# Output weights of a hybrid decoder step: split on chip one stage earlier, tokens' blocks stored by tiles, the samples' steps moved forward

## The chip, the cores and the metric

One core of a Trainium2 chip runs the whole kernel. The metric is the device time of one execution in microseconds; with one core that is the core's own time. The engines are TensorE (PE, matmuls), VectorE (DVE), ScalarE (ACT), GpSimd (POOL) and SyncE (SP, which here issues the DMAs). Each runs its own instruction stream strictly in order, and they meet only at semaphores.

## The reference, cut to what matters

Two layers over a prompt of 2048 tokens, and in the same launch one decode step for 8 samples (1 token each, with their own caches). All fp32.

```
D_MODEL 1024, D_MAIN 1024, D_MEMW 512 (4 heads of 128, 256 memory slots), D_CAT 1536, WINDOW 128
for l in (0, 1):
    u, g_main, q_mem, g_mem = split(rmsnorm(x) @ w_in[l])          # 1024 -> 3072
    l == 0: y = rglru(causal_conv4(u))                             # gates by 64x64 block diagonals, linear scan
    l == 1: k, v = rmsnorm(x) @ w_kv; y = sliding_window_gqa(rope(u), rope(k), v, sinks)
    om = softmax(q_mem @ mem_k[l].T) @ mem_v[l]
    z = concat(y * silu(g_main), om * silu(g_mem))                 # 1536
    x = x + z @ w_out[l]                                           # 1536 -> 1024
return rmsnorm(x), and the states and caches (of the prompt and of the samples)
```

## The kernel before, in words

Every large fp32 product is made of three matmuls on rounded halves: with a = a_hi + a_lo and b = b_hi + b_lo (ACT copies to the rounded type, DVE or POOL subtracts for the low part) it sums hi·hi, hi·lo and lo·hi. All PE times below are those of such triples. The program of each engine is written out by hand: stage functions loop over chunks of 512 tokens (`q` counts them) and call hooks of the neighbouring stages (`ahead[...]`), so that work of the next stage is issued between the chunks of this one. A wait stands in the queue of its engine until it is met, and everything behind it stands too.

Stages in order of time: memory keys and values; layer 0's items (`mem_*`, then `lru_*`, the recurrence stage: chunks q = 0 to 33, 12.2 us each, four chunks for each block of 256 weight columns, an "item"); the output product of layer 0 (`output(l=0)`, PE at L2098); layer 1's keys and values, memory items and window attention; and last `paired`, the output product of layer 1 (L2661).

**Recurrence stage.** SP's order in a chunk is `lru_sp` (L1024): tiles, `sums_sp`, weights, rows, then every fourth chunk the load of an item's weights (1 MB, L571) and of the gates' blocks, then the store of a finished z chunk (L677) and of the samples' row. The item's weights are wanted by PE at the second chunk of the next item, for the samples' row of the projection (`project_samples`, L628). ACT's order is `lru_act`: root, weight halves, branch copy, tiles, tanh and exp, gate copy, then `ahead["weights_act"]`. Beside it `block_sums` (L2694) prepares sums of blocks of w_out for the last stage: a step loads two rows of blocks (L2715), POOL makes four sums in place (L2725 to L2730), SP stores them (L2719). There are 6 steps, each over two chunks: in an even chunk SP waits for the previous store to land and issues the loads, in the odd chunk it waits for POOL and stores. From chunk 28 on SP also loads the output weights of layer 0 in thirds (L1782), ACT splits them (L1787).

**Last stage.** The product 1536 -> 1024 is split in two phases f of 768 rows each, and in each phase the 2x2 block product (tokens x rows by rows x columns) is made by seven products of blocks (Winograd's form), of 3 x 3 matmuls of 128x128 by 128x512, about 2.05 us each, in the order P2, P1, P4, P6, P5, P7, P3. A unit is 256 tokens of one phase: units 0 to 7 are phase 0, units 8 to 15 phase 1, and units 0 and 1 are partly woven into the end of the window attention (`tail`; first P2 and P1 of unit 0). For a unit SP loads z in four blocks (A22, S2 = A21, A11, A12; L2284) and x or the partial result (L2293); POOL makes S1, S3, S2, S4 from them (L2402 to L2409); ACT rounds the first three blocks and then the other four (L2440, L2443); DVE makes the low parts in three pieces (L2527), and adds each product from its bank to the rows (L2541). A product may start when the bank was added two products ago (`product`, L2640). In phase 0 the rows go back to DRAM (`store_x`, L2327), in phase 1 they are normalised and stored as the result (`store_y`). z of a unit takes the buffer of the unit two before, and is loaded when that unit's P6 is done. z lies in DRAM as (12, 128, 2048), so a load of a tile is made of pieces of 512 B. The products' weights are loaded raw (a block of w_out, or a sum), rounded by ACT (L2434) and split by DVE (L2520; POOL for P3, L2414): for phase 0 in chunks 29 to 32 of the window stage, for phase 1 in units 3 to 9.

Between the products of units 9 to 13 PE, DVE, ACT and POOL do the window attention of the 8 samples in six steps (`sm[...]`): SP loads rows, keys (L1452) and values (L1476), PE's window scores are L1532. At the end the samples' z is multiplied by w_out, which SP loads again in two halves (`again`, L2336; PE at L2671).

SP's order in a unit is `sync` (L2338): z of the next unit, store of the previous rows (only from unit 9 here), x of the next unit, special loads, and in units 1 to 7 the store of this unit's rows at its end.

## Time and profile before

| | |
|---|---|
| time, median of 3 runs | 2081.75 us (2080.78 to 2083.16) |
| the profiled execution: time, span | 2081.3 us, 2079.5 us |
| PE busy | 2025.7 us (97%), 14353 matmuls |
| DVE, ACT, POOL busy | 1293.0 (62%), 951.7 (46%), 240.0 us (12%) |
| mean granted clock of TensorE | 0.988 of full speed |
| last stage's matmuls, L2661 | 404.6 us in 1008 matmuls, 27.0 us of idle before them |
| DMA | 244.76 MB, 118 GB/s over the span, 251 in the busiest late slice |

The span runs from the first to the last instruction of the profiled execution; the time of that execution is 1.8 us more. With PE busy for 97% of it, what an edit can give is the idle time of PE and the time in which its clock was granted at half.

### The profile page before, as it was taken

Reading aid. Unit: us, or ns where it says so; the run is one execution under the profiler, and the core shown is the slowest. Engines: PE = TensorE matmul, PEld = TensorE weight load, DVE = VectorE, ACT = ScalarE, POOL = GpSimd, SP = SyncE. Lnnn points to the kernel's source line nnn. Section 1 sums busy time; section 2 is a strip of 40 time slices with the busy share of each in tenths; the row PEclk is TensorE's granted clock in tenths of the full one; section 3 lists DMA queues with packets and bytes.
Section 4 is the critical chain, followed back from the end, with each engine's and each line's share of the span. In section 5 each row is a group of like instructions: output and inputs, shape, how many; then the busy total and the mean of one; then the engine's idle time right before and its main releaser. Section 6 shows DMA issues by size and latency. Waiting matters only on the chain.

```text
span 2079.5 us, 34876 instructions
## 1 busy us (share of the span) xinstructions
PE 2025.7 (97%) x14353; PEld 1604.3 (77%) x14353; DVE 1293.0 (62%) x2165; ACT 951.7 (46%) x2061; POOL 240.0 (12%) x232
## 2 busy tenths in 40 slices
PE   9999999999999999999999999999999998998995
PEld 8788887777777787777888888777777887776763
DVE  5745437887777832223634444688888889865764
ACT  6633335777777823222533333444444445223431
POOL 0000001320000000000200000222222220223310
PEclk9999999999999999999999999999999999999997
DMA  9311113332111465453211111212222215467674
GB/s 385 138 64 46 62 45 120 129 126 71 45 45 56 160 211 187 147 169 126 79 44 43 37 43 49 80 50 85 70 85 70 85 63 174 170 231 267 221 251 180
DMA packets 133119, 244.76 MB, mean 118 GB/s; under 512 B 14340, under 2 KB 69668, under 8 KB 128472
## 3 DMA queue, kind: packets, MB, share of 16 engines
q1 hardware_dynamic: 132960, 242.54, 34.2%
q8 instruction: 113, 1.85, 0.4%
q14 instruction: 46, 0.38, 0.1%
HBM read 179.40 MB, written 63.16 MB: 117 GB/s over the span
## 4 chain that ended last, share of the span: by engine, by line
PE 85%; DVE 5%; DMA 4%; SPq 2%; issue 2%; POOL 1%; ACT 1%; DVEq 0%; POOLq 0%
PE bank L608 52%; PE bank L2098 12%; PE bank L2661 4%; PE bank L150 2%; PE bank L712 2%; PE bank L1173 2%; PE bank L448 2%; PE bank L1159 2%; PE bank L699 2%; DMA op_zraw<-z_scratch 2%; PE bank L908 1%; SPq L2284 1%; PE bank L628 1%; DVE op_x L2541 1%; PE bank L702 1%
## 5 line engine op out<-in xcount | busy, mean ns | idle before, releaser
L608 PE MATMUL bank<-x_hi,w_hi 128*128 128x512 f32 x1600 | 636.2, 398 | 0.4 <-DVE w_lo L594 0.4
L608 PE MATMUL bank<-x_hi,w_lo 128*128 128x512 f32 x1600 | 624.1, 390 | 0.0
L608 PE MATMUL bank<-x_lo,w_hi 128*128 128x512 f32 x1600 | 623.1, 389 | 0.0
L608 PEld LDWEIGHTS bank<-x_hi,w_hi 128*128 128x128 f32 x1600 | 300.1, 188 | 96.7 <-issue 35.4
L608 PEld LDWEIGHTS bank<-x_hi,w_lo 128*128 128x128 f32 x1600 | 300.3, 188 | 64.6
L608 PEld LDWEIGHTS bank<-x_lo,w_hi 128*128 128x128 f32 x1600 | 300.5, 188 | 60.8 <-issue 0.7
L2661 PE MATMUL bank<-op_whi_p,op_zhi 128*128 128x512 f32 x336 | 136.9, 407 | 27.0 <-DVE op_x L2541 12.6
L2098 PE MATMUL bank<-wo_hi,z_hi 128*128 128x512 f32 x384 | 151.8, 395 | 1.1 <-DVE z_lo L1821 1.1
L2098 PE MATMUL bank<-wo_lo,z_hi 128*128 128x512 f32 x384 | 149.7, 390 | 0.0
L2098 PE MATMUL bank<-wo_hi,z_lo 128*128 128x512 f32 x384 | 149.5, 389 | 0.0
L758 DVE TENSOR_TENSOR it_P_lo<-bank,it_P_hi 128x512 fp32r<-128x512 f32 x64 | 41.2, 686 | 161.6 <-ACT it_P_hi L753 161.6
L1211 ACT ACTIVATE it_X<-it_X,stat 128x128 f32<-128x128 f32 x256 | 99.2, 389 | 91.9 <-DVE stat L1280 91.9
L653 ACT ACTIVATE it_gh<-bank 128x512 f32<-128x512 f32 x96 | 56.8, 592 | 180.7 <-PE bank L608 180.7
L2661 PE MATMUL bank<-op_whi_p,op_zlo 128*128 128x512 f32 x336 | 134.0, 399 | 0.0
L2661 PE MATMUL bank<-op_wlo_p,op_zhi 128*128 128x512 f32 x336 | 133.7, 398 | 0.0
L1337 POOL TENSOR_SCALAR w_raw<-w_raw,prm 128x256 f32<-128x256 f32 x56 | 59.8, 1069 | 546.0 <-PE bank L628 275.3
L2541 DVE TENSOR_TENSOR op_x<-op_x,bank 128x512 f32<-128x512 f32 (+1 forms) x112 | 84.8, 759 | 53.5 <-PE bank L2661 53.2
L1247 DVE TENSOR_TENSOR it_PTs<-bank,tmask 128x512 f32<-128x512 f32 x128 | 79.4, 682 | 57.4 <-PE bank L150 57.2
L2661 PEld LDWEIGHTS bank<-op_whi_p,op_zhi 128*128 128x128 f32 x336 | 64.9, 193 | 45.8 <-issue 18.9
L747 ACT ACTIVATE it_Pm<-bank,stat 128x256 f32<-128x256 f32 x128 | 59.0, 474 | 88.0 <-DVE stat L766 88.0
L2098 PEld LDWEIGHTS bank<-wo_hi,z_hi 128*128 128x128 f32 x384 | 72.0, 188 | 21.3 <-issue 3.8
L586 ACT ACTIVATE w_hi<-w_raw,prm 128x256 fp32r<-128x256 f32 x200 | 85.1, 507 | 0.3 <-PE bank L702 0.3
(363 smaller groups left out, 3216.0 us busy)
## 6 DMA issues: line engine op xcount, KB each, us to landing
w_raw<-in_w_items SPq DMA_DIRECT2D x25, 1024.0 KB, 5.1
z_scratch<-it_gz SPq DMA_DIRECT2D x96, 256.0 KB, 2.6
it_cs<-in_rope SPq DMA_DIRECT2D x32, 512.0 KB, 4.1
op_x<-x_scratch SPq DMA_DIRECT2D x32, 512.0 KB, 4.9
z_raw<-z_scratch SPq DMA_DIRECT2D x16, 768.0 KB, 5.7
op_zraw<-z_scratch SPq DMA_DIRECT2D x64, 192.0 KB, 4.1
in_rows<-in_x_prompt SPq DMA_DIRECT2D x4, 2048.0 KB, 26.7
in_x<-in_x_T SPq DMA_DIRECT2D x4, 2048.0 KB, 27.3
```

The costliest lines, as they stand in the source:

```text
L150: last = nc.tensor.transpose(banks[a][:, 64 * i:64 * i + 64], of(i)[e, :], ident[e, e])
L448: last = nc.tensor.matmul(mk_bank(i)[:, 256 * h:256 * h + 256], s_, r_, start=(k == 0), stop=(k == KT - 1))
L586: nc.scalar.activation(m.w_hi[w % 2][:, k, :], m.w_raw[w % 2][:, k, :], ACT.Copy, scale=m.prm[:, k, gain(w):gain(w) + 1]).then_inc(S["w_hi ...
L608: last = nc.tensor.matmul(ps, s_, r_, start=(k == 0 and q == 0), stop=(k == KT - 1 and q == 2))
L653: nc.scalar.activation(gh[:, :], PG, ACT.Copy, scale=0.5)
L747: nc.scalar.activation(Pm[:, t, :], (S0, S1)[t // 2][:, (t % 2) * M:(t % 2 + 1) * M], ACT.Exp, bias=negm[:, t:t + 1], scale=MEM_SCALE, acc ...
L1211: e = nc.scalar.activation(X[:, j, :], X[:, j, :], ACT.Exp, bias=negm[:, j:j + 1], accum_out=rs[:, j:j + 1])
L1247: r = nc.vector.tensor_tensor(PTs[:, h, a, :].rearrange("p (t b k) -> p t b k", t=4, b=2), by_halves(m.psum, 6, h), m.tmask[:, a, :].rearr ...
L1337: nc.gpsimd.tensor_scalar(raw, raw, m.prm[:, k, gain(w):gain(w) + 1], None, ALU.mult).then_inc(S["zeros"], 1)
L2098: last = nc.tensor.matmul(bank(t, h), s_, r_, start=(first and q == 0), stop=(end and q == 2))
L2541: nc.vector.tensor_tensor(x, x, y, ALU.add).then_inc(xn, 1)
L2661: last = nc.tensor.matmul(bank(u, i), s_[:, k, :], r_[:, k, :], start=(i not in (P6, P7, P3) and k == 0 and q == 0), stop=(k == KQ - 1 and ...
```

## The change

- **Splitting ahead.** `block_sums` now makes a step in every chunk (q = 3 to 8: wait for POOL, store, wait for the landing, load the next) and then, from chunk 8 on, the high and low parts of all 21 weight blocks of phase 0, in pairs over two chunks each: load raw, ACT copies (hook behind `weights_act`), POOL subtracts, SP stores. In the last stage the weights of phase 0 are loaded as two finished parts (`load_w`, f = 0), and their splits on ACT (21), DVE (18) and POOL (3) are gone there.
- **z by tiles.** z's DRAM buffer is (16, 128, 12, 128); a tile's load is contiguous for each partition, a chunk's store is in pieces of 512 B.
- **Order of SP's queue.** z(u+1) is issued ahead of the row stores of unit u-1 and in pieces, each when the product that last read its buffer is done; x(0) goes ahead of P5's weights, P3's parts behind z(1); row stores of units 1 to 7 come after the next z; in phase 1 the weights P7 get a buffer of their own and are loaded in unit 6; the samples' values go behind the rows in unit 10 and not 11; w_out is loaded again in units 12 and 13 and not 13 and 14.
- **DVE and ACT order.** Tokens' low parts of unit 0 move from behind the window stage's last normalisation to before it; P7's round copy goes ahead of the tokens' of unit 9.
- **Samples' steps.** The six steps are moved forward by three to nine products on PE and DVE.

```diff
-        self.z_d = nc.dram_tensor("z_scratch", (NI, 128, T), F32).ap()
+        self.z_d = nc.dram_tensor("z_scratch", (TT, 128, NI, 128), F32).ap()
...
-        s.dma_start(m.z_d[item(kind, i, p) - l, :, c * CH:(c + 1) * CH], gz[g % NG][:, :]).then_inc(stored[g % NG], 16)
+        s.dma_start(m.z_d[4 * c:4 * c + 4, :, item(kind, i, p) - l, :].rearrange("t p e -> p t e"), gz[g % NG][:, :].rearrange("p (t e) -> p t e", t=4)).then_inc(stored[g % NG], 16)
...
             ahead["weights_act"](act, q)
+            ahead["sums_act"](act, q)
...
-        s.dma_start(m.z_raw[slot(t)][:, :, :], m.z_d[:, :, t * 128:(t + 1) * 128].rearrange("k p t -> p k t")).then_inc(z_ld[t % 2], 16)
+        s.dma_start(m.z_raw[slot(t)][:, :, :], m.z_d[t]).then_inc(z_ld[t % 2], 16)
...
+             [V0, V0 + 12 * KB, V0 + 24 * KB, V0 + 36 * KB, WS + 16 * KB, LO + 54 * KB, WS]]
+    at_hi = [[at_lo[f][i] + 6 * KB for i in range(NPROD)] for f in range(2)]
+    at_hi[0][P3], at_hi[1][P7], at_hi[1][P3] = LO + 48 * KB, HI + 21 * KB, HI + 33 * KB
...
     def load_w(s, f, i):
         on, value = loaded[f][i]
+        if f == 0:
+            s.wait_ge(on, value - 32)
+            for part, to in enumerate((w_hi, w_lo)):
+                s.dma_start(to[0][i][:, :, :].bitcast(F32), sums["split"](part, KQ * i, KQ).rearrange("k p n -> p k n")).then_inc(on, 16)
+            return
         s.wait_ge(on, value - 16)
...
     def load_z(s, u):
         f, j, p = phase(u), u % 8, u % 2
         it["z_stored"](s, NCH * (6 * f + 5) + j // 2)
-        if u >= 2:
-            s.wait_ge(mmd, MM0 + made(u - 2, P6))
-        k = 6 * f
-        for e, k, h in ((A22, k + 3, 1), (S2, k, 1), (A11, k, 0), (A12, k + 3, 0)):
-            s.dma_start(z_raw[p][:, e, :, :], m.z_d[k:k + KQ, :, 256 * j + 128 * h:256 * j + 128 * h + 128].rearrange("k p t -> p k t")).then_inc(z_ld[p], 16)
+        for i, e, k, h in ((P2, A12, KQ, 0), (P1, A11, 0, 0), (P4, A22, KQ, 1), (P6, S2, 0, 1)):
+            if u >= 2:
+                s.wait_ge(mmd, MM0 + made(u - 2, i))
+            s.dma_start(z_raw[p][:, e, :, :], m.z_d[2 * j + h, :, 6 * f + k:6 * f + k + KQ, :]).then_inc(z_ld[p], 16)
...
         if q == 31:
             s.wait_ge(*chunk_free(2))
             load_w(s, 0, P6)
+            load_x(s, 0)
             load_w(s, 0, P5)
-            load_x(s, 0)
             load_w(s, 0, P7)
-            load_w(s, 0, P3)
     def late_sp(s, q):
         if q == 32:
             s.wait_ge(*chunk_free(3))
             load_z(s, 1)
+            load_w(s, 0, P3)
             load_x(s, 1)
...
     def sync(s):
-        for u in range(1, UNITS):
-            if 2 <= u < UNITS - 1:
+        for u in range(2, UNITS):
+            if u < UNITS - 1:
                 load_z(s, u + 1)
-            if u >= 9:
+            if u <= 8:
+                store_x(s, u - 1)
+            else:
                 store_y(s, u - 1)
-            if 2 <= u < UNITS - 1:
+            if u < UNITS - 1:
                 load_x(s, u + 1)
             if u == 2:
                 s.wait_ge(*after("z_ready", NI * NCH))
...
             if u in (3, 4, 5):
                 load_w(s, 1, (P1, P4, P6)[u - 3])
             if u == 6:
+                s.wait_ge(*chunk_free(3))
+                load_w(s, 1, P7)
+            if u == 7:
                 load_w(s, 1, P3)
-            if u == 7:
                 s.wait_ge(mmd, MM0 + made(7, P2))
                 load_w(s, 1, P5)
-            if u < 8:
-                store_x(s, u)
             if u == 8:
-                s.wait_ge(mmd, MM0 + made(7, P7))
-                load_w(s, 1, P7)
                 s.wait_ge(mmd, MM0 + NPROD * 8)
                 sm["sp"](s, 0)
                 sm["sp_keys"](s)
             if u == 10:
                 sm["sp"](s, 1)
-            if u == 11:
                 sm["sp"](s, 2)
-            if u == 13:
+            if u == 12:
                 s.wait_ge(sm["signals"]["pv_d"], 2)
                 again(s, range(0, 8, 2))
+            if u == 13:
+                s.wait_ge(sm["zs_r"], sm["zs_0"] + 3)
+                again(s, range(8, NI, 2))
             if u == 14:
                 s.wait_ge(sm["zs_r"], sm["zs_0"] + 3)
                 sm["sp"](s, 6)
-                again(s, range(8, NI, 2))
                 s.dma_start(x_s[0:NS, :], m.x1_d[TT * 128:TA, :]).then_inc(x_ld[2], 16)
...
     def pool(g):
-        sums_tokens(g, 0)
-        sums_tokens(g, 1)
-        low_pool(g, 0)
-        for u in range(2, UNITS):
+        for u in range(UNITS):
             sums_tokens(g, u)
             if u == 9:
-                low_pool(g, 1)
-            if u == 10:
+                for k in range(KQ):
+                    g.wait_ge(whi, W0 + KQ * P3 + k + 1)
+                    nc.gpsimd.tensor_tensor(w_lo[1][P3][:, k, :], w_raw[1][P3][:, k, :], w_hi[1][P3][:, k, :].bitcast(F32), ALU.subtract).then_inc(wlop, 1)
                 sm["pool"](g)
...
     def within_act(act, q):
-        if q in (29, 30):
-            weights_act(act, 0, (P2, P1)[q - 29])
         if q == 31:
             for n in range(2):
                 tokens_act(act, 0, n)
         if q == 32:
             tokens_act(act, 1, 0)
-            weights_act(act, 0, P7)
-            weights_act(act, 0, P3)
...
+            if u == 8:
+                weights_act(act, P7)
             if 2 <= u + 1 < UNITS:
                 tokens_act(act, u + 1, 0)
             if u == 8:
-                for i in (P7, P3):
-                    weights_act(act, 1, i)
+                weights_act(act, P3)
                 nc.scalar.activation(st[:, 63:64], m.eps, ACT.Sqrt, bias=m.eps, scale=1.0)
             if u < UNITS - 1:
                 tokens_act(act, u + 1, 1)
             if 3 <= u < 8:
-                weights_act(act, 1, (P2, P1, P4, P6, P5)[u - 3])
-            if 9 <= u < 13:
-                sm["act"](act, (0, 1, 2, 4)[u - 9])
+                weights_act(act, u - 3)
+            if u == 9:
+                sm["act"](act, 0)
+            if u == 10:
+                sm["act"](act, 1)
+                sm["act"](act, 2)
+            if u == 12:
+                sm["act"](act, 4)
...
     def within_dve(v, q):
         if q == 31:
-            weights_low(v, 0, P4)
+            for n in range(2):
+                tokens_low(v, 0, n)
         if q == 32:
-            weights_low(v, 0, P7)
             add(v, 0, P5)
             tokens_low(v, 1, 0)
     def result_dve(v, q):
+        if q == 31:
+            tokens_low(v, 0, 2)
         if q == 32:
             add(v, 0, P7)
     def behind_dve(v, q):
-        if q in (29, 30):
-            weights_low(v, 0, (P2, P1)[q - 29])
-        if q == 31:
-            for n in range(3):
-                tokens_low(v, 0, n)
         if q == 32:
             tokens_low(v, 1, 1)
             add(v, 0, P3)
+            tokens_low(v, 1, 2)
...
-                if (u, i) == (9, 0):
+                if (u, i) == (8, 6):
                     sm["sum_rows"](v, c)
...
-                step = {(9, 6): 0, (10, 5): 1, (11, 3): 2, (12, 2): 3, (12, 6): 4, (13, 3): 5}.get((u, i))
+                step = {(9, 3): 0, (10, 2): 1, (10, 6): 2, (11, 5): 3, (12, 1): 4, (12, 5): 5}.get((u, i))
...
-            if u % 8 == 0:
-                pe.wait_ge(*((wlop, WP0 + KQ * f + k + 1) if i == P3 else (wlo, W0 + low_at(f, i, k))))
+            if u == 0 and k == 0:
+                pe.wait_ge(*loaded[0][i])
+            if u == 8:
+                pe.wait_ge(*((wlop, WP0 + k + 1) if i == P3 else (wlo, W0 + KQ * i + k + 1)))
...
-                step = {(9, 2): (0, 1), (10, 1): (1, 1), (10, 2): (1, 2), (10, 3): (1, 3), (11, 1): (2, 3), (12, 0): (3, 3), (12, 4): (4, 3), (13, 1): (5, 3)}.get((u, i))
+                step = {(9, 0): (0, 1), (9, 5): (1, 1), (9, 6): (1, 2), (10, 0): (1, 3), (10, 5): (2, 3), (11, 3): (3, 3), (11, 6): (4, 3), (12, 3): (5, 3)}.get((u, i))
...
+    s_d = nc.dram_tensor("split_scratch", (2, NB, 128, 512), F32).ap()
...
+    blocks = [block[k][i] for i in range(7) for k in range(KQ)]
+    PAIRS_ = [range(n, min(n + 2, NB)) for n in range(0, NB, 2)]
+    Q0 = 2 + NT
+    def keep(s, q):
+        if 3 <= q <= Q0:
+            l, f, k = STEPS[q - 3]
+            s.wait_ge(made, 4 * (q - 2))
+            s.dma_start(t_d[l, f, :, k].rearrange("j p e -> p j e"), b[:, :, :]).then_inc(kept, 16)
+            s.wait_ge(kept, 16 * (q - 2) + 16)
+        if q > Q0 and (q - Q0) % 2 == 0 and (q - Q0) // 2 <= len(PAIRS_):
+            n = (q - Q0) // 2 - 1
+            js = PAIRS_[n]
+            s.wait_ge(made, 4 * NT + 2 * n + len(js))
+            for part, x in enumerate((hi, lo)):
+                s.dma_start(s_d[part, js[0]:js[0] + len(js)].rearrange("j p e -> p j e"), x[:, 0:len(js), :].bitcast(F32)).then_inc(kept, 16)
+            s.wait_ge(kept, 16 * NT + 32 * (n + 1) + 16)
     def sp(s, q):
+        keep(s, q)
+        if 2 <= q < Q0:
+            l, f, k = STEPS[q - 2]
+            for j in range(2):
+                s.dma_start(b[:, 2 * j:2 * j + 2, :], A["w_out"][l, 6 * f + KQ * j + k].rearrange("p (j e) -> p j e", j=2)).then_inc(got, 16)
+        elif q >= Q0 and (q - Q0) % 2 == 0 and (q - Q0) // 2 < len(PAIRS_):
+            for j, n in enumerate(PAIRS_[(q - Q0) // 2]):
+                s.dma_start(raw[:, j, :], blocks[n]).then_inc(got, 16)
+    def act(act, q):
+        n = (q - Q0) // 2
+        if q > Q0 and (q - Q0) % 2 == 1 and n < len(PAIRS_):
+            act.wait_ge(got, 16 + 32 * NT + 32 * n + 16 * len(PAIRS_[n]))
+            for j in range(len(PAIRS_[n])):
+                nc.scalar.activation(hi[:, j, :], raw[:, j, :], ACT.Copy).then_inc(high, 1)
...
+        for n in range(NB):
+            g.wait_ge(high, 16 + n + 1)
+            tt(lo[:, n % 2, :], raw[:, n % 2, :], hi[:, n % 2, :].bitcast(F32), ALU.subtract).then_inc(made, 1)
...
```

## Rows read from the trace of the kernel before

**Rows 1.** Waits of PE, 1600 to 2080 us: engine, line, releaser: total, times, longest.

```profile
PE bank L2671 <- DMA op_w_again<-in_w_out: 15.7, 1, 15.7
PE bank L2661 <- DVE op_x L2541: 12.6, 3, 7.2
PE bank L2661 <- issue: 8.5, 1, 8.5
PE bank L2661 <- DVE op_zlo L2527: 4.9, 4, 1.7
```

**Rows 2.** Timeline of PE: start, duration, what [idle before, releaser].

```profile
1802.99 0.50 PE L2661 MATMUL bank<-op_whi_p,op_zhi 128*128 128x512 f32 x1
...
1901.25 0.50 PE L2661 MATMUL bank<-op_whi_p,op_zhi 128*128 128x512 f32 x1 [0.81 <-DVE op_zlo L2527]
```

**Rows 3.** Recurrence stage: timelines of SP, POOL, PE, and landings of L2719 and L571.

```profile
337.63 0.93 SPq L2715 DMA_DIRECT2D sums<-in_w_out  x2
...
342.69 1.75 POOL L2725 TENSOR_TENSOR sums<-sums 128x512 f32<-128x512 f32 x1 [30.79 <-DMA sums<-in_w_out]
...
349.30 0.38 SPq L2719 DMA_DIRECT2D sums_scratch<-sums  x1
...
DMA to landing us min/median/max: 4.0/4.2/4.8
...
409.72 0.33 SPq L571 DMA_DIRECT2D w_raw<-in_w_items  x1
...
DMA to landing us min/median/max: 5.0/5.0/5.0
...
428.22 1.07 PE L628 MATMUL bank<-w_raw,xsg 128*32 128x256 f32 x16
```

**Rows 4.** Around the stage change: SP, landings of L1782, ACT and DVE.

```profile
681.84 0.38 SPq L1782 DMA_DIRECT2D wo_raw<-in_w_out  x1
...
DMA to landing us min/median/max: 8.0/9.0/9.7
...
682.82 3.90 ACT L1787 ACTIVATE wo_hi<-wo_raw 128x1024 fp32r<-128x1024 f32 x4
...
694.97 3.90 ACT L1787 ACTIVATE wo_hi<-wo_raw 128x1024 fp32r<-128x1024 f32 x4
...
703.22 1.76 DVE L1821 TENSOR_TENSOR z_lo<-z_raw,z_hi 128x1536 fp32r<-128x1536 f32 x1 [0.29 <-ACT z_hi L1817]
```

**Rows 5.** Last stage's start: DVE, SP, and a window (PE to POOL, clock, DMA, GB/s).

```profile
1760.03 1.89 DVE L2520 TENSOR_TENSOR op_wlo_p<-op_wraw_p,op_whi_p 128x512 fp32r<-128x512 f32 x3
...
1766.88 1.22 DVE L1290 TENSOR_TENSOR it_X<-it_X,stat 128x1024 f32<-128x1024 f32 x1
...
1768.63 3.09 DVE L2527 TENSOR_TENSOR op_zlo<-op_zraw,op_zhi 128x1152 fp32r<-128x1152 f32 x3
...
1766.99 2.02 SPq L2284 DMA_DIRECT2D op_zraw<-z_scratch  x4
...
1752.00:1758.00 6.00, 5.99 (x99) 4.64 (x98) 6.00 (x10) 4.05 (x4) 0.00 (x0) 1.00 0.99 280
```

**Rows 6.** Timeline of DVE in unit 4.

```profile
1852.63 1.36 DVE L2527 TENSOR_TENSOR op_zlo<-op_zraw,op_zhi 128x1152 fp32r<-128x1152 f32 x1 [3.43 <-POOL op_zraw L2409]
```

**Rows 7.** From unit 8 on: SP, two windows, POOL and PE.

```profile
1906.96 0.81 SPq L2293 DMA_DIRECT2D op_x<-x_scratch  x2
...
1915.12 3.81 SPq L1452 DMA_DIRECT2D sm_k<-in_cache_mem_k  x8
...
1919.20:1923.00 3.80, 3.80 (x9) 3.02 (x10) 3.71 (x3) 3.44 (x4) 3.80 (x3) 0.50 1.03 410
1930.60:1932.40 1.80, 1.80 (x11) 1.44 (x9) 1.76 (x4) 0.00 (x0) 0.00 (x0) 1.00 1.13 297
...
1934.26 1.41 POOL L2402 TENSOR_TENSOR op_zraw<-op_zraw 128x384 f32<-128x384 f32 x1 [10.22 <-DMA op_zraw<-z_scratch]
...
1944.89 1.95 PE L1532 MATMUL bank<-sm_qs,sm_kw 64*128 64x8 f32 x16
```

103 lines of the change are left out of this document (39 added, 64 removed).

## The prediction

> **What bounds the kernel now.** I read the waits of PE first, then PE's own timeline, then, at each place where PE stands, the timeline of the engine it waits for and SP's queue. Of the 2079.5 us span PE stands still for some 47 us in pieces over 0.3 us, and all but four of them lie in the last stage, the paired output product (L2661), as [rows 1] shows: 15.7 us for the last re-load of weights, 12.6 us for DVE additions, 8.5 us at the stage's start (put down as "issue", the wait for the first split tokens), 4.9 us for split tokens at unit starts. A long idle costs again afterwards: the granted clock is 0.50 from 1919.2 to 1923.0, after the 7.2 us gap before 1919.12 [rows 7]; half rate for some 4 to 5.5 us is 2 to 2.8 us per gap. Everywhere else PE has no gap, so what SP, ACT, DVE and POOL do there is free until it makes PE wait. The stage gives at most 43 us plus 8 of slow clock. [Rows 2] fix its time line: P5 of unit 1 starts at 1802.99, unit 8 at 1901.25, so 45 products take 98.3 us, 4.9 of them idle, 2.05 to 2.08 each.
>
> **Part 1, splitting ahead, in the recurrence stage.** The additions to ACT (21 copies) and POOL (21 subtractions) are hidden by their idle time in that stage. The order of SP's queue is not. Before, a step of the block sums takes two chunks: loads in one, store in the next. Now each chunk q from 3 to 8 first waits for POOL, stores, waits until the store has landed, and only then loads and goes on to the rest. One step in [rows 3]: loads at 337.63, POOL starts at 342.69 (5.1), four operations, store at 349.30 (6.6), landed 4.0 to 4.8 later: 15.8 us, against 12.2 us for a chunk. SP runs late by 3.6 more at every step: the sixth store has landed at 337.6 + 6 x 15.8 = 432.4, with the two raw loads (0.9) and some queueing the weights of item 7 are issued at 433.8, not 409.72, and land 5.0 plus 1.2 (half a MB ahead of them) later, at 440. PE wants them at 428.22 for the samples' row (L628). Stall 11.6, slow clock 2.4: **+14.0**. Bounds: 0 if the slack holds (it ends at an issue before 422), 18 if DVE's gate ring, whose store of z is as late, adds its own.
> After that each pair takes two chunks. At every fourth chunk SP waits for ACT's copies, POOL (2 x 1.7), a landing (4.2) and issues two loads; the item's weights go out 5.2 us after the gates' matmuls instead of 5.3 before them and land at 11.4, wanted at 13.2. Nothing, by 1.8 us.
> The 21st block is the exception. Its copy stands on ACT behind the split of the output weights, which ends at 682.82 + 3.90 = 686.7 [rows 4]. POOL is done at 689.0, the store has landed at 692.4, and only now SP issues the second third of the output weights, 681.84 before. It lands 8.0 to 9.7 later: 700.7, so ACT's second group starts 5.7 later than 694.97, and DVE, which at 703.22 waits directly for ACT, and is full from there to PE's gap at 724.8, passes it on. **+6.0**, between 3 (if the store lands at once and the load in 7) and 9 (clock).
>
> **Part 2, the stage's start.** DVE loses 18 weight splits here and POOL the three of P3 (DVE's take 0.63 each, three in 1.89); tokens' low parts move from behind the normalisation (1768.63) to 1760.03 [rows 5]. P2 and P1 run from 1761.6 instead of 1770.1. But flip 30 needs the normalisation, which stays where it is: 0.4 us more work before it, 1.4 less before that. PE waits 2.3 there. Then the loads: P6, P5 and P7 are now two parts of 0.79 MB each, 5.8 MB with the row blocks, at 280 GB/s: until 1774. z(1), at 1766.99 before and 1765.5 now, stands behind them and lands at 1776.6; POOL's sums take 4.7 and DVE stands until 1781.3 before the part it needs. P3's parts land at 1782.3, PE waits 2.6 more, then 1.1 for an addition. P5 of unit 1 starts at 1796.3 instead of 1802.99: **-6.7**. With data at 350 GB/s it is -9.4; with the loads another 3 us late, -3.5.
>
> **Part 3, units 2 to 7.** z(u+1) leaves before the row stores, piece by piece as P2, P1, P4, P6 of unit u-1 end, some 8 us earlier. DVE's 3.43 us wait for POOL's sums [rows 6], seen once a unit, has over 8 us of cover. Adds of a unit still fit DVE (10 of 14.3). All 4.9 go, and the slower first product after each: **-6.0** (-4.9 to -6.4).
>
> **Part 4, unit 8 to the end.** 178.25 us before (1901.25 to 2079.5). P7's weights are there already, so its 7.2 us goes. What is next? Count from unit 8's start, distances in [rows 7]. x(9) leaves at 4.1 (5.7 before), rows and window, then eight keys from 11.6 (13.9). 5.2 MB at 410 GB/s end at 24.7. z(10) stands behind them, in pieces of 1.5 KB instead of 512 B: 0.79 MB between 297 and 410 GB/s, 2.3 us; landed at 28 (33.0 before). ACT takes z(10) and its sums before the samples' step 0, and that step now stands in DVE behind P6 of unit 9, PE's window scores behind P7. From z(10)'s landing (1934.26) to the scores (1944.89) are 10.6 us, 1.2 of them other work of DVE: scores at 28 + 9.4 = 37.4. PE is there at 13 x 2.05 + 0.3 = 27.0. **Stall 10.4**, which did not exist, since three products more lay before it. From there to unit 12: 15 products 31.2, samples' matmuls and transposes 13.7, clock 2.3, two waits of 1.2 and 0.9 for additions behind steps 1 and 2. The values' 4.2 MB are now ahead of z(12): values land at +47.1, z(12) at +49.4, DVE stands for its sums at +54, with step 3 behind it; PE waits 3.2 and 6.2. Together 58.7. Units 12 and 13: 29.1, transposes 0.8, clock 2.4, z(14) behind 4.2 MB of re-loaded weights 2.8: 35.1. Unit 14 and the samples' product: 14.4 + 5.9, the 15.7 us wait gone because both re-loads leave a unit earlier. From there 21.5 as before. 37.4 + 58.7 + 35.1 + 20.3 + 21.5 = 173.0: **-5.3**. The bounds: +3 if z(10), z(12), z(14) each land 3 us later; -20 if no samples' step makes PE wait (10.4 + 9.4 less what is there anyway).
>
> [...]
>
> The rows have z at 297 GB/s in 512 B pieces and keys at 410 in 4 KB ones [rows 7]. The Trainium skill (DMA: Bandwidth & Descriptors, Specifications) puts the least size for line rate at 512 B. By it z by tiles would save nothing, z(10), z(12) and z(14) would each land 0.4 us later than I have them, and the sum would be 1.2 higher; the trace does not bear the rule out.
>
> **Sum.** 14.0 + 6.0 - 6.7 - 6.0 - 5.3 = +2.0: span 2081.5, with 1.8 around it 2083.3. The profiled run (2081.3) lies 0.45 under the median 2081.75, so the time is 2083.8.
>
> **Rivals.** (a) SP's lateness is absorbed in the recurrence stage: the weights at chunk 8 land in time. For it: DVE and ACT have some 8 us of lead over PE; against: this load has no lead beyond 6 us and the chain is in-order. 2083.8 - 14.0 = 2069.8. (b) The samples' steps don't stall PE in units 9 and 11, because z lands early: 2083.8 - 10.4 - 2.3 - 6 = 2065. Against: the queue is at 410 GB/s, full. (c) Slower: the weights of each item at chunks 12, 16, 20, 24, which I have landing 1.8 us before PE wants them. It decides from a landing 1.9 us later than mine: POOL beside a busy DVE (the operation on 128x512 took 1.75 us), two landings in a row. At 3 us per item and its ACT work, four items: 2083.8 + 12 = 2096. (d) The splits don't do what they say (P2 and P1 still late at 1770): +8, 2092.
>
> **Chances.** Forecast 0.52 (own range 2077 to 2090), (a) 0.15, (b) 0.12, (c) 0.15, (d) 0.06. What can be told from no change is 0.2%, 4.2 us. Of the forecast's 0.52, 0.09 is below 2077.6, 0.22 within, 0.21 above. Faster 0.09 + 0.15 + 0.12 + 0.01 = 0.37; same 0.23; slower 0.21 + 0.15 + 0.04 = 0.40. The range reaches to (a)'s and (c)'s numbers and a little past: 2067 to 2096.
>
> **What would show it.** A PE gap of 11 to 12 us before the samples' row of chunk 9 (428 us, L628), with a clock of 0.5 behind it; a new wait of DVE or PE around 718 to 745. In the last stage: no gap before P2 of unit 0, none for split tokens at unit starts, none at P7 of unit 8; one of about 10 us before the window scores in unit 9 and one before the window values in unit 11, each behind a z load in SP's queue; none before the last unit. If the first gap is missing the time falls to (a); if every fourth chunk has one, (c). If the recurrence stage is clean and the last one keeps its 43 us, everything here is wrong.

## The result, and the profile after

The changed kernel takes 2090.7 us (median of 5 runs, 2086.1 to 2093.1) against 2081.3 (5 runs, 2078.5 to 2083.2): ratio 1.0041, interval 1.0028 to 1.0054. It is 0.4% slower. The profiled execution took 2091.7 us, its span is 2089.9, so 10.4 us more than before.

PE's waits in the whole run (engine, line, what it waited for: us in total, times, longest); the lines that answer to [rows 1] are L2652 (once L2661) and L2662 (once L2671, no wait any more):

```profile
PE bank L1533 <- DVE sm_kw L1646: 7.0, 1, 7.0
PE bank L2652 <- DVE op_zlo L2524: 5.9, 1, 5.9
PE bank L628 <- DMA w_raw<-in_w_items: 5.8, 1, 5.8
PE bank L608 <- DVE w_lo L594: 4.2, 2, 3.7
PE bank L2099 <- DVE z_lo L1822: 4.1, 2, 2.9
PE bank L1574 <- DMA sm_v<-in_cache_mem_v: 3.9, 1, 3.9
PE bank L1582 <- DVE sm_wpT L1702: 3.7, 1, 3.7
PE bank L2652 <- DVE op_x L2538: 2.4, 3, 0.8
```

Four of these groups did not exist before (L1533, L628, L1574, L1582); the single 5.9 us wait for tokens, before unit 14, and the 3.7 us at L608 are new in their places. Starts of the same instructions on PE in both timelines cut the run into stretches (us):

| stretch | before | after | difference | forecast |
|---|---|---|---|---|
| start to the samples' row of 329 us | 329.1 | 330.3 | +1.2 | 0 |
| to the samples' row of 626 us (recurrence stage) | 297.4 | 312.3 | **+14.9** | +14.0 |
| to the first samples' matmul of layer 1 (stage change, output product) | 408.8 | 412.8 | **+4.0** | +6.0 |
| to P2 of unit 0 | 734.8 | 726.0 | -8.8 | } -6.7 |
| to P5 of unit 1 | 32.9 | 33.4 | +0.5 | } |
| to unit 8 | 98.3 | 91.9 | **-6.3** | -6.0 |
| unit 8 to the end | 178.2 | 183.3 | **+5.0** | -5.3 |

The first line is chance: over all traces of this study that point lies between 329.1 and 331.7. The recurrence stage, as PE, SP, DVE and POOL show it (start, duration, line, what [idle before, releaser]; the lines that answer to [rows 3]):

```profile
338.82 0.93 SPq L2725 DMA_DIRECT2D sums<-in_w_out  x2
350.48 0.38 SPq L2710 DMA_DIRECT2D sums_scratch<-sums  x1
354.51 0.83 SPq L2725 DMA_DIRECT2D sums<-in_w_out  x2
...
407.58 1.05 DVE L666 SCALAR_TENSOR_TENSOR it_gz<-it_gth,it_gh 128x512 f32<-128x512 f32 x1 [3.41 <-DMA z_scratch<-it_gz]
...
417.01 1.67 DVE L594 SCALAR_TENSOR_TENSOR w_lo<-w_raw,prm,w_hi 128x256 fp32r<-128x256 f32 x4
417.54 0.79 PE L608 MATMUL bank<-x_hi,w_hi 128*128 128x512 f32 x1 [3.73 <-DVE w_lo L594]
...
429.99 0.38 SPq L2710 DMA_DIRECT2D sums_scratch<-sums  x1
434.91 0.43 SPq L571 DMA_DIRECT2D w_raw<-in_w_items  x1
...
441.99 1.93 PE L628 MATMUL bank<-w_raw,xsg 128*32 128x256 f32 x16 [5.81 <-DMA w_raw<-in_w_items]
442.95 0.69 DVE L666 SCALAR_TENSOR_TENSOR it_gz<-it_gth,it_gh 128x512 f32<-128x512 f32 x1 [7.68 <-DMA z_scratch<-it_gz]
```

A step takes 15.7 us from load to next load (338.82 to 354.51), as forecast, the sixth has its store out at 430.0, and the item's weights leave at 434.9. Two waits follow: the one forecast (5.8 us at L628) and one before it (3.7 at 417.5) for low parts that stand in DVE behind waits for a gate buffer, whose store of z SP issues late. The 3.41 in the DVE row at 407.58 is such a wait; from its end to the low parts at 417.01 DVE has no pause. In the whole run DVE waits 40.0 us (9 times) for these stores, before never. The 7.68 in the last row is another.

The stage change (SP, ACT and PE; answers to [rows 4]). The stage starts 16.0 us later than before, so the second third of the output weights, out at 681.84 before, would be due at 697.9:

```profile
707.33 0.38 SPq L1783 DMA_DIRECT2D wo_raw<-in_w_out  x1
715.46 3.91 ACT L1788 ACTIVATE wo_hi<-wo_raw 128x1024 fp32r<-128x1024 f32 x4 [3.83 <-DMA wo_raw<-in_w_out]
725.01 0.50 PE L2099 MATMUL bank<-wo_hi,z_hi 128*128 128x512 f32 x1 [2.88 <-DVE z_lo L1822]
```

The last stage (PE, SP, POOL, DVE; the first two rows answer to [rows 2], the others to [rows 7]):

```profile
1814.72 0.50 PE L2652 MATMUL bank<-op_whi_p,op_zhi 128*128 128x512 f32 x1
1906.66 0.40 PE L2652 MATMUL bank<-op_whi_p,op_zhi 128*128 128x512 f32 x1
1917.54 3.94 SPq L1453 DMA_DIRECT2D sm_k<-in_cache_mem_k  x8
1921.58 1.81 SPq L2290 DMA_DIRECT2D op_zraw<-z_scratch  x4
1934.06 1.02 POOL L2409 TENSOR_TENSOR op_zraw<-op_zraw 128x384 f32<-128x384 f32 x1 [7.06 <-DMA op_zraw<-z_scratch]
1941.82 0.01 DVE L1641 LOAD_MASK_SELECT sm_qr<-sm_q  x1 [9.25 <-ACT sm_gth_s L1605]
1942.98 3.55 PE L1533 MATMUL bank<-sm_qs,sm_kw 64*128 64x8 f32 x16 [7.04 <-DVE sm_kw L1646]
```

Unit 8 starts 91.9 us after P5 of unit 1 (98.3 before). z(10) leaves behind the keys, is there at 1934.1, and the scores start 36.3 us after unit 8. What came after that wait is in the granted clock (window: its length, PE, PEld, DVE, ACT, POOL busy (x), clock, DMA share, GB/s):

```profile
1942.00:1946.00 4.00, 3.02 (x15) 3.05 (x15) 3.89 (x15) 0.00 (x0) 2.08 (x2) 0.50 0.32 118
1946.00:1950.00 4.00, 4.00 (x11) 3.24 (x12) 2.89 (x3) 2.68 (x4) 1.99 (x2) 0.50 0.02 4
1950.00:1955.00 5.00, 5.00 (x20) 4.28 (x19) 1.79 (x2) 3.52 (x6) 1.00 (x1) 0.50 0.00 0
1955.00:1960.00 5.00, 5.00 (x36) 2.98 (x39) 0.69 (x1) 1.68 (x2) 0.00 (x0) 0.60 0.00 0
```

PE is busy and at half rate (1.2 GHz) from 1943 to 1959. The clock had fallen at 1938.5 already, while PE stood.

### The profile page after: what moved, and what is told of

Same layout as the page of the kernel before. It is cut to its first block, busy times and chain, and to the rows that moved or that the text cites. A ratio compares the mean times of both kernels' runs of the same rounds, so it can differ in the third digit from the quotient of the medians.

```text
span 2089.9 us, 34924 instructions
## 1 busy us (share of the span) xinstructions
PE 2038.9 (98%) x14353; PEld 1613.8 (77%) x14353; DVE 1277.1 (61%) x2147; ACT 948.4 (45%) x2059; POOL 264.9 (13%) x250
## 4 chain that ended last, share of the span: by engine, by line
PE 86%; DMA 5%; DVE 3%; POOL 2%; ACT 1%; issue 1%; SPq 0%; DVEq 0%; POOLq 0%
PE bank L608 47%; PE bank L2099 12%; PE bank L2652 9%; PE bank L150 2%; PE bank L712 2%; PE bank L1174 2%; PE bank L448 2%; PE bank L1160 2%; DMA op_zraw<-z_scratch 2%; PE bank L699 2%; DMA sums<-in_w_out 1%; DMA sums_scratch<-sums 1%; PE bank L628 1%; PE bank L908 1%; PE bank L702 1%
## 5 line engine op out<-in xcount | busy, mean ns | idle before, releaser
L608 PE MATMUL bank<-x_hi,w_hi 128*128 128x512 f32 x1600 | 637.9, 399 | 4.2 <-DVE w_lo L594 4.2
L608 PE MATMUL bank<-x_hi,w_lo 128*128 128x512 f32 x1600 | 625.5, 391 | 0.0
L608 PE MATMUL bank<-x_lo,w_hi 128*128 128x512 f32 x1600 | 624.6, 390 | 0.0
L608 PEld LDWEIGHTS bank<-x_hi,w_hi 128*128 128x128 f32 x1600 | 301.1, 188 | 101.7 <-issue 35.8
L608 PEld LDWEIGHTS bank<-x_hi,w_lo 128*128 128x128 f32 x1600 | 301.2, 188 | 64.7
L608 PEld LDWEIGHTS bank<-x_lo,w_hi 128*128 128x128 f32 x1600 | 301.5, 188 | 61.0 <-issue 0.7
L2652 PE MATMUL bank<-op_whi_p,op_zhi 128*128 128x512 f32 x336 | 137.1, 408 | 8.7 <-DVE op_zlo L2524 5.9
L2652 PE MATMUL bank<-op_wlo_p,op_zhi 128*128 128x512 f32 x336 | 134.6, 401 | 0.0
L2652 PE MATMUL bank<-op_whi_p,op_zlo 128*128 128x512 f32 x336 | 134.3, 400 | 0.0
L666 DVE SCALAR_TENSOR_TENSOR it_gz<-it_gth,it_gh 128x512 f32<-128x512 f32 x96 | 74.3, 774 | 46.4 <-DMA z_scratch<-it_gz 40.0
```

The lines of the kernel that those rows point to most:

```text
L608: last = nc.tensor.matmul(ps, s_, r_, start=(k == 0 and q == 0), stop=(k == KT - 1 and q == 2))
L666: nc.vector.scalar_tensor_tensor(gz[g % NG][:, :], gth[:, :], 1.0, gh[:, :], ALU.add, ALU.mult).then_inc(S["gz_free"], 1)
L2652: last = nc.tensor.matmul(bank(u, i), s_[:, k, :], r_[:, k, :], start=(i not in (P6, P7, P3) and k == 0 and q == 0), stop=(k == KQ - 1 and ...
```

## The experiments

Each run stands with the kernel before on the same chip, where that took 2080.5 to 2082.0 us; "less" is against the changed kernel's 2090.7, which was measured where the kernel before took 2081.3, so such differences carry about 1 us of that.

**1. Item's weights ahead of the sums.**

```diff
         for q in range(NL + 2):
+            if q < NL and q % 4 == 0:
+                i, p, c = LRU[q]
+                w = item("main", i, p)
+                if w + 1 < NW:
+                    s.wait_ge(S["g_done"], B["g_done"] + NCH * w)
+                    load_w(s, w + 1)
             ahead["tiles_sp"](s, q)
             ahead["sums_sp"](s, q)
...
```

> The changed kernel with one move in the recurrence stage: SP issues an item's weights ahead of the block sums' step of that chunk, not behind it. In the changed kernel's trace the step of chunk 8 holds SP until 434.9 us, the item's weights land at 441.9 and PE waits 5.8 us for them; before that, PE waits 3.7 us for low parts that stand in DVE behind a wait for a store of z. Theory A (the item's weights behind the step are the whole cost): both waits go, with the slow clock behind them, about -14 us. Theory B (SP is late as a whole, and the stores of z, which free the gates' buffers for DVE, are as late as the weights): only the wait at the samples' row goes, 5.8 plus its share of slow clock; the low parts' wait of 3.7 stays and DVE still waits 3 to 8 us for stores: -6 to -9 us. I expect B. Nothing else in the run should move by more than 1 us.

2080.8 us (ratio to before 1.0001, 0.9991 to 1.0010), 9.9 less. The recurrence stage takes 304.4 us, 7.9 less. SP and PE:

```profile
419.50 0.50 SPq L571 DMA_DIRECT2D w_raw<-in_w_items  x1
...
417.99 0.80 PE L608 MATMUL bank<-x_hi,w_hi 128*128 128x512 f32 x1 [4.03 <-DVE w_lo L594]
436.49 1.07 PE L628 MATMUL bank<-w_raw,xsg 128*32 128x256 f32 x16
```

Theory B: the wait at L628 and its slow clock go, the other stays at 4.0, and half of the loss with it. SP is late as a whole. That nothing else would move by more than 1 us did not hold: from unit 8 to the end this profile is 3.6 us shorter than the changed kernel's, with the same program there and 1.8 us more of waits. After the 6.8 us wait before the window scores the clock is back at 1.00 within 6.3 us here (and at half once more from 1945.5 to 1949.0), there within 16.0.

**2. Steps spread out.** Half chunks h are counted; a step is load, store two later, next load three later; pairs of splits from h = 22 on, in four.

```diff
+            ahead["sums_act"](act, q)
             ahead["weights_act"](act, q)
-            ahead["sums_act"](act, q)
...
-            ahead["sums_sp"](s, q)
+            ahead["sums_sp"](s, 2 * q)
...
+            ahead["sums_sp"](s, 2 * q + 1)
...
-            s.wait_ge(kept, 16 * (q - 2) + 16)
...
+    H0, H1 = 4, 4 + 3 * NT
...
+        n, r = divmod(h - H0, 3)
+        if 0 <= n < NT:
...
+            if r == 0:
+                if n:
+                    s.wait_ge(kept, 16 * n + 16)
...
+            if r == 2:
+                s.wait_ge(made, 4 * (n + 1))
...
+        n, r = divmod(h - H1, 4)
...
```

> The changed kernel with the block sums' six steps over one and a half chunks each (load, store a chunk later, next load half a chunk after that) and the eleven splits over two chunks each from chunk 11 on, so that SP finds POOL done and the store landed and does not stand; ACT's copies of a pair go ahead of the output weights' split, not behind it. My theory (all of the 14.6 us that the recurrence stage lost is SP standing in the steps, and the 4.0 us at the stage change is the last block's copy behind the output weights' split): no wait of PE at 410 to 445 us, none for output weights around 715 to 745, -14.6 and -4.0, together about -18 us, 2072. Rival (contention: the sums and splits slow POOL and DVE, or the added 22 MB of transfers slow the loads, so that part of it stays however they are spread): half of it, -5 to -12. A further danger: the last splits now lie in chunks 29 to 33 beside the output weights' loads and may move the stage change by up to +5.

2071.7 us (0.9949, 0.9935 to 0.9964), 19.0 less. The recurrence stage takes 297.40 us, to the hundredth what it took before, though the same 22.0 MB more are moved as in the changed kernel (266.8 MB by its page, 244.8 before) and the same copies and subtractions are made: it was SP standing, not contention. PE at the same place:

```profile
429.04 1.07 PE L628 MATMUL bank<-w_raw,xsg 128*32 128x256 f32 x16
```

No wait, and the slow clock went with it. The stage change gives back 1.9 of its 4.0 (410.9 us); waits of 0.8 for the output weights' low parts and 1.2 for z are left. That ACT's copy moved and that SP stands less came together there, so which of them gave the 1.9, and what holds the rest, stays open. From P2 of unit 0 to unit 8 this profile is 1.6 us shorter than the changed kernel's, in which the clock was at half from 1788.3 to 1791.7; here it was not.

**3. z(10) ahead of the keys.**

```diff
-            if u < UNITS - 1:
+            if u < UNITS - 1 and u != 9:
                 load_z(s, u + 1)
...
                 sm["sp"](s, 0)
+                load_z(s, 10)
                 sm["sp_keys"](s)
```

> The changed kernel with z of unit 10 issued ahead of the samples' eight key blocks in SP's queue, not behind them. In the changed kernel z(10) is landed at 1934.0 us, ACT's copy of the samples' row stands behind that unit's tokens, PE waits 7.0 us before the window scores, and the granted clock is 0.5 from about 1938 to 1957. My theory (queue order): z(10) lands about 10 us earlier, the wait goes and with it the slow clock behind it (10 us of it, over which PE was busy for most): -12 to -17 us. Rival (the samples' steps stand too close: PE would wait for the chain row, flip, ACT, DVE even with z there): the wait shrinks to 2 to 4 us and the clock still falls, -3 to -6. The keys land some 3 us later, which nothing waits for.

2080.2 us (0.9991, 0.9981 to 1.0000), 10.5 less in the medians. The profiled execution is the slowest of the ten (2084.4), its span 7.3 less, and of that 6.3 lie in unit 9. PE, and two windows:

```profile
1937.39 2.65 PE L1533 MATMUL bank<-sm_qs,sm_kw 64*128 64x8 f32 x16 [1.66 <-DVE sm_kw L1646]
```

```profile
1943.00:1949.00 6.00, 6.00 (x22) 5.00 (x22) 1.74 (x2) 3.29 (x6) 4.57 (x4) 0.50 0.02 6
1949.00:1955.00 6.00, 6.00 (x67) 3.50 (x69) 0.69 (x1) 2.77 (x2) 0.10 (x1) 0.75 0.00 0
```

Neither theory has it right. The queue made the wait, which falls from 7.0 to 1.7 us; but the clock still halves behind 1.7 us. The shortfall (half of the time at 0.50) is 6.8 us, all of it while PE works; before this edit it was 10.2, of which 2.2 fell while PE stood, so 8.0 cost time.

**4. The samples' steps back at their old products.**

```diff
-                step = {(9, 3): 0, (10, 2): 1, (10, 6): 2, (11, 5): 3, (12, 1): 4, (12, 5): 5}.get((u, i))
+                step = {(9, 6): 0, (10, 5): 1, (11, 3): 2, (12, 2): 3, (12, 6): 4, (13, 3): 5}.get((u, i))
...
```

> The changed kernel with the samples' steps (PE, DVE and ACT) back at the products where they stood before; every load stays in the changed kernel's order. Theory A (the steps moved closer are what makes PE wait for loads: 7.0, 3.9 and 3.7 us and slow clock behind each): with three to nine more products ahead of each step these waits go, and only the re-loaded output weights could come late, since the samples' z is ready five products later: -10 to -15 us. Theory B (the loads' order alone matters, the waits only move: DVE's tokens for units 10, 12 and 14 stand behind z loads that stand behind 4.2 MB, whoever asks for them): unit starts 10, 12 and 14 wait 3 to 6 us each instead, -3 to +3 us. I expect something between, nearer to A: -8.

2074.3 us (0.9963, 0.9951 to 0.9976), 16.4 less. (PE's table and ACT's calls go back with DVE's.) Unit 8 to the start of the last product takes 157.4 us in place of 174.3 (169.2 before the change). Theory A, and twice what I gave it: the moved steps alone turned the last stage from a gain into a loss. One wait is new (PE, and ACT before it):

```profile
1989.49 0.79 PE L2647 MATMUL bank<-op_whi_p,op_zhi 128*128 128x512 f32 x1 [12.60 <-DVE op_x L2533]
...
1980.46 1.16 ACT L2440 ACTIVATE op_zhi<-op_zraw 128x1152 fp32r<-128x1152 f32 x1 [11.66 <-DMA op_zraw<-z_scratch]
```

ACT waits for z(12), which stands behind 4.2 MB of values; the samples' exponential (L1625) stands behind ACT's copies, and in DVE, which waits 13.8 us for it, the additions stand behind that.

**5. Close steps, loads in order** (z(10) before the keys, values right behind z(11), re-loads behind z(14)).

```diff
-            if u < UNITS - 1:
+            if u < UNITS - 1 and u != 9:
                 load_z(s, u + 1)
+            if u == 10:
+                sm["sp"](s, 2)
...
+                load_z(s, 10)
                 sm["sp_keys"](s)
             if u == 10:
                 sm["sp"](s, 1)
-                sm["sp"](s, 2)
-            if u == 12:
+            if u == 13:
                 s.wait_ge(sm["signals"]["pv_d"], 2)
                 again(s, range(0, 8, 2))
-            if u == 13:
```

> The changed kernel with three loads moved in SP's queue and the samples' steps left close: z(10) ahead of the keys (as in the run before, which took 6.3 us out of unit 9), the values as soon as the memory scores are done in unit 10 (ahead of the row stores, so some 15 us earlier than now and well ahead of z(12)), and both re-loads of the output weights behind z(14). Theory A (the close steps cost only by the order of the loads): the waits for values (3.3 to 3.9), for the window values' chain (3.7) and for the tokens of unit 14 (5.5 to 5.9) all go with their slow clock: some -15 more, 2066 to 2070 in all. Theory B (the steps' own chains, PE to DVE to ACT and back, are longer than the products between them): the waits move to the flips and the scores, and of the 15 us half stays, 2072 to 2078. I expect B for the first steps and A for the last: 2070.

2079.6 us (0.9993, 0.9983 to 1.0002), 11.1 less, slower than either theory's number. The waits for values, for the window values' chain and for tokens go; in their place are 8.6 us behind additions (2.4 in the changed kernel), 4.3 for the re-load, and 6.8 of slow clock from unit 9 on as in run 3.

**6. Old steps, loads in order** (z(10), keys; z(12), values, small rows; z(14), re-loads).

```diff
+                load_z(s, 10)
                 sm["sp_keys"](s)
             if u == 10:
+                load_z(s, 12)
+                sm["sp"](s, 2)
                 sm["sp"](s, 1)
-                sm["sp"](s, 2)
...
```

> The changed kernel with the samples' steps at their old products (as in the run before, 16.9 us less in the last stage) and in SP's queue z(10) ahead of the keys, z(12) ahead of the values, the values ahead of the small window rows, and both re-loads behind z(14). In the run before two waits were left, 4.3 us for the tokens of unit 10 and 12.6 us behind ACT, whose copy of tokens for unit 12 stood behind 4.2 MB of values; the clock was 0.5 for 20 us of the stage. Theory: both waits are queue order alone, so unit 8 to the end takes 157.4 - 4.3 - 12.6 and about 5 of slow clock = 135 to 138 us, the whole kernel 2074.3 - 21 = 2053. Rival: the values are then what PE waits for at unit 12 (they can't leave before the memory scores are done, and need 10 us for 4.2 MB): a wait of 4 to 8 us with its clock, 2060 to 2064.

2068.7 us (0.9937, 0.9923 to 0.9952), 22.0 less: the rival, in another place than it said. The two waits are gone (unit 11 takes 15.4 us, 29.6 in run 4), but x(12) is late behind the small rows, for whose landing SP stands, and PE waits 4.8 us for the addition that needs it; the re-load is 4.2 us late. DVE at that place:

```profile
1982.18 1.41 DVE L2534 TENSOR_TENSOR op_x<-op_x,bank 128x512 f32<-128x512 f32 x2 [6.08 <-DMA op_x<-x_scratch]
```

**7. Runs 2 and 6 together** (both diffs, nothing else).

> Both mends together: the spread steps and splits of the recurrence stage (measured alone: 19 us less than the changed kernel) and the old steps with the loads in the order z, keys, z, values, z, re-loaded weights. They lie 1200 us apart and share no queue state, so they should add up: the other mended kernel of this call less 17 to 19 us, 2034 to 2038 if that one comes to 2053. If it comes to more than 3 us off that sum, something from the first stage reaches into the last, which would be new.

2052.0 us (0.9858, 0.9843 to 0.9872), 16.7 less than run 6 where 17 to 19 were expected (run 2 alone gave 19.0): they add up to within 2.3 us. That it isn't 2034 to 2038 is run 6's own miss.

**8. z's layout as before.**

```diff
-        self.z_d = nc.dram_tensor("z_scratch", (TT, 128, NI, 128), F32).ap()
+        self.z_d = nc.dram_tensor("z_scratch", (NI, 128, T), F32).ap()
...
```

> The changed kernel with z's DRAM buffer as before, (12, 128, 2048): loads of a tile in pieces of 512 B, stores of a chunk in pieces of 2 KB; everything else stays. Theory A (pieces of 512 B move at 297 GB/s against 410, as the rows of before have it): each z load of units 10, 12 and 14, which PE waits for, lands 0.8 us later, the sum +2 to +3 us against the changed kernel; in units 2 to 7 nothing, since z has 8 us of lead. Theory B (512 B is enough for line rate): no difference anywhere in the last stage. A third: the stores in 512 B pieces of the changed kernel are what costs (the gates' buffers come free later in the recurrence stage), so that this run is faster there by 0.5 to 2 us. I expect A, by a difference that the total can hardly show and the landings in the trace can.

2092.0 us (1.0047, 1.0032 to 1.0062), 1.3 more, which the total can't tell from nothing. The landings can (the page's DMA issues: count, KB each, median us to landing; first the changed kernel, then this one):

```profile
z_raw<-z_scratch SPq DMA_DIRECT2D x16, 768.0 KB, 5.0
op_zraw<-z_scratch SPq DMA_DIRECT2D x64, 192.0 KB, 6.4
```

```profile
z_raw<-z_scratch SPq DMA_DIRECT2D x16, 768.0 KB, 5.6
op_zraw<-z_scratch SPq DMA_DIRECT2D x64, 192.0 KB, 6.9
```

Half a microsecond each: theory A's mechanism at about its size (0.5 where it said 0.8). The third theory falls: the recurrence stage takes 313.0 us here against 310.8 to 312.3 in five traces with tiles (the changed kernel, runs 3 to 6), so it isn't shorter, and the median landing of z's stores there is 2.8 us here, 2.7 in the changed kernel.

**9. The kernel before with z ahead of the row stores alone.**

```diff
-        if u >= 2:
-            s.wait_ge(mmd, MM0 + made(u - 2, P6))
...
+            if 2 <= u < 9:
+                s.wait_ge(mmd, MM0 + made(u - 2, i))
...
                 load_z(s, u + 1)
+            if 2 <= u <= 8:
+                store_x(s, u - 1)
...
-            if u < 8:
-                store_x(s, u)
```

> The kernel before with one part of the change alone: z(u+1) is issued ahead of the row stores of unit u-1, in pieces as the products of that unit end, for units 3 to 8; layout, weights, samples and everything from unit 8 on stay as before. Theory: PE's waits for split tokens at the starts of units 5 to 8 (4.9 us) go with the slower first products, units 2 to 7 take 85.7 us in place of 92.0, and the total falls by 6.3 us (2075), if unit 8 on keeps its 178 us. Rival: the layout in tiles does it (pieces of 1.5 KB, sooner landed), and the order alone leaves 1 to 3 us of it: 2078. A second rival: row stores later mean x comes later (each x load waits until the store of two units ago has landed), and the wait moves to DVE's additions: no gain.

2070.8 us (0.9953, 0.9937 to 0.9969), 9.7 less than before. Units 2 to 7 take 85.68 us, the same as in the changed kernel, without tiles and without split weights. (The order in the queue and the loading in pieces came together; they were not parted.) From unit 8 to the start of the last product this one is 5.1 us shorter as well (164.1 against 169.2), which I had not expected: the 7.2 us wait at P7 of unit 8 is 4.4, with less slow clock behind it. The row store of unit 7 no longer stands in front of P7's weights in SP's queue; that this is the reason was not tested.

**10. The best version.** As run 7, with the small window rows behind x(12), and the first 4.2 MB of re-load right behind z(14).

```diff
                 load_z(s, u + 1)
+            if u == 13:
+                s.wait_ge(sm["signals"]["pv_d"], 2)
+                again(s, range(0, 8, 2))
...
+            if u == 11:
                 sm["sp"](s, 1)
             if u == 13:
-                s.wait_ge(sm["signals"]["pv_d"], 2)
-                again(s, range(0, 8, 2))
```

> The best kernel so far (2052.0: spread steps, old samples' steps, loads in order) with two more moves in SP's queue: the small window rows, for whose landing SP stands until 1954, go behind x(12), which DVE waited 4.9 us for (PE 3.5 us); and the first 4.2 MB of re-loaded output weights go right behind z(14), ahead of the row store, so that the last 2.1 MB land before PE wants them and z(15) is not 18 us under way. Theory: the 3.5 us wait goes with 1.7 us of slow clock; the 4.2 us wait for re-loaded weights, the 0.9 us for tokens and the 2.6 us behind the samples' additions in unit 15 go with theirs: -8 to -12 us, 2041 to 2044. Rival: the values' 4.2 MB, z(12) and z(14) fill the queues, so that the re-load ahead of x(14) makes x(14) late in its turn: 2 to 4 us of DVE wait at unit 14, -5.

2042.3 us (0.9810, 0.9791 to 0.9830): 38 us under the kernel before (2080.5 on this chip), 48 under the changed one. The waits in unit 12 and for the re-load are gone, and one of 3.7 us for an addition in unit 14 has come, where the rival put it. Its profiled execution is its slowest (2048.6); the others are 2039.4 to 2042.4. The granted clock accounts for most of it (PE and a window of this run, then PE and a window of run 7 for the same scores):

```profile
1928.54 0.50 PE L2651 MATMUL bank<-op_whi_p,op_zhi 128*128 128x512 f32 x1 [1.26 <-DVE op_x L2537]
1931.48 3.58 PE L1534 MATMUL bank<-sm_qs,sm_kw 64*128 64x8 f32 x16
```

```profile
1930.00:1935.00 5.00, 5.00 (x21) 4.16 (x19) 3.01 (x4) 1.16 (x1) 2.97 (x3) 0.50 0.30 121
```

```profile
1928.58 1.95 PE L1534 MATMUL bank<-sm_qs,sm_kw 64*128 64x8 f32 x16
```

```profile
1928.00:1934.00 6.00, 6.00 (x52) 4.46 (x54) 3.04 (x5) 1.88 (x2) 4.80 (x4) 1.00 0.43 175
```

Behind a wait of 1.3 us, three microseconds ahead of the scores, they and the product behind them run at half rate; in run 7, which has no such wait there, at full. Unit 10, in which this lies, takes 28.4 us here and 22.4 in the profiles of runs 7 and 11.

**11. The same without splitting ahead.**

```diff
-    return dict(sp=sp, act=act, pool=pool, made=made, total=4 * NT + NB, of=of, split=lambda part, n, w: s_d[part, n:n + w])
+    return dict(sp=sp, pool=pool, made=made, total=4 * len(STEPS), of=lambda l, f, j: t_d[l, f, j])
...
-        if f == 0:
-            s.wait_ge(on, value - 32)
-            for part, to in enumerate((w_hi, w_lo)):
...
```

> As the other mended kernel of this call, but without splitting ahead: block sums as in the kernel before, and the weights of phase 0 loaded raw, rounded by ACT and split by DVE and POOL in the window stage's end; z by tiles, the order of loads and the samples' steps are the mended ones. It tells what splitting ahead is worth once it costs nothing in the recurrence stage. From the traces of the kernel before and of the run with spread steps: the last stage's start takes 112.7 us against 104.1 up to P2 of unit 0 and 32.9 against 33.4 from there, the stage change 2.1 us less: so this one is slower by 8.6 - 0.5 - 2.1 = 6.0 us (2048 if the other is 2042). Rival: the re-ordered loads alone mend part of the start, and the difference is under 2 us.

2047.6 us (0.9842, 0.9824 to 0.9861), 5.3 more than run 10, 6.0 forecast. The two intervals overlap (four executions each, and run 10's lie 9 us apart), so the medians alone don't settle it. The profiles do for the stages that the edit touches: the recurrence stage takes 297.40 us in both, from its end to P2 of unit 0 1143.5 us in place of 1136.9, from there to unit 8 125.5 in place of 125.3. Splitting ahead is worth 6.7 us there, once the recurrence stage is spread to carry it.

## Why the prediction was right, and where it wasn't

The time lies in the range and on the side forecast: 2083.8, measured 2090.7, slower. Of its five terms four hold to 2 us or less; the last has the wrong sign. It is 10.3 us too low; with 1.2 of chance at the start, less 3.0 by which the other four together came out lower than said, that is the 8.4 us between the spans (+2.0 forecast, +10.4 measured), 6.9 in the medians.

Two things in this are luck. The measured time lies just outside the forecast's own range (2077 to 2090) and inside the whole one (2067 to 2096) only because that reaches to rival (c), which did not happen; part 4's own upper bound was +3. And the side was nearly even, 0.40 slower against 0.37 faster: with part 4 as said the kernel would have come out within noise of no change.

- **Part 1, +14.0: right** (14.9). The mechanism (SP 3.6 us later at each step, measured 3.5; the item's weights out at 433.8, measured 434.9) stands, and run 2 shows that it is all. But its path was told too short. I had the loss as one wait of 11.6 us at L628 (by its own numbers, 440 less 428.22, it is 11.8), and named the gates' ring as a bound only; it is two waits, 3.7 behind the ring and 5.8 at L628, with slow clock at each (3.4 us of shortfall both times, 0.7 and 1.0 of it while PE still stood): 3.7 + 2.7 + 5.8 + 2.4 = 14.6 of the 14.9. Run 1 separates them: taking the weights out of the queue saves 7.9, not 14. Rival (a) is out, as is (c): no item from chunk 12 on made PE wait.
- **The 21st block, +6.0: right in kind, a third too large** (4.0). The second third of the output weights left 9.4 us late (10.6 said), ACT's second group started 4.5 late (5.7 said), and PE waited 2.9 and 1.2 for z's low parts (once 1.1 before).
- **Part 2, -6.7: right** (-8.3). P2 of unit 0 is 8.8 earlier (8.5 said), flip 30 waits 2.0 (2.3 said), so rival (d) is out. The 2.6 us wait for P3's parts did not come; the one for an addition did, 0.8 (1.1 said).
- **Part 3, -6.0: right** (-6.3), by the order of the queue and the loading in pieces alone (run 9).
- **Part 4, -5.3: wrong** (+5.0), by 10.3 us.
  - To the scores 37.4, measured 36.3, with a wait of 7.0 for 10.4.
  - From there to unit 12 58.7, measured 64.8: of it 44.9 are products and the samples' matmuls at full rate, 9.2 are waits (3.9 + 3.7 + 0.7 + 0.8; I had 11.5 with the additions), and so 10.7 are slow clock where the sum has **2.3**. That is the term which failed. The granted clock agrees: in this stretch its shortfall while PE worked is 11.3 us, 8.0 behind the 7.0 us wait and some 3 behind the two later ones.
  - I took half rate from [rows 7], 4 to 5.5 us of it behind a gap, but there PE goes on with 128x512 products; behind this gap it goes on with the samples' 64x8 matmuls, and the clock is 0.50 until 1959. (That the small matmuls are the reason was not isolated. Runs 3 and 10 show the same after shorter waits near the same place. But run 1, which has the changed kernel's last stage and a wait of 6.8 us at this point, lost 4.9 us to the clock behind it and not 8.0, and took 61.3 us from the scores to unit 12 and not 64.8: the price also varies between executions, and a part of the 10.7 is of this one.)
  - Units 12 and 13: 35.1, measured 38.5, since the tokens of unit 14 came 5.9 us late behind the re-loaded weights and not 2.8. Unit 14 and the samples' product 20.3, measured 22.1, slow clock again. 36.3 + 64.8 + 38.5 + 22.1 + 21.5 = 183.2 (183.3 before rounding).
- Runs 3 and 4 show what the part did not say. Removing the queue's share (run 3) leaves a 1.7 us wait and most of the slow clock (6.8 of the 8.0 us that cost time); giving the steps their products back (run 4) takes 16.9 us out. I had counted that the steps would stall PE, and set the stall against the waits that went, 7.2 and 15.7, as if it cost little more than its own length.
- **512 B pieces.** The sentence from the Trainium skill (DMA: Bandwidth & Descriptors, Specifications), by which z in tiles saves nothing, is not borne out by the landings (5.0 and 6.4 us against 5.6 and 6.9, run 8); the total is 1.3 us apart, so it decided nothing here.

## What to carry to other kernels

A helper that waits for its own round trip (load, compute, store, landing) inside a shared in-order DMA queue makes everything behind it as late as it is, each time; place each of its waits half a chunk to a chunk after what it waits for, and the same work is free (run 2: 14.9 us, with nothing left out). Put small loads with a near deadline ahead of bulk ones, and ask of each bulk load which engine's next instruction stands behind it. Before steps are moved closer, price a stall with the clock at half over what PE does next, not with its length.
